# Half of the first layer's cross values computed between the output projection and the expert choice, with the bias table's write and the router's VectorE order moved

## The chip, the cores and the metric

One Trainium2 chip, one of its cores. The metric is the device time of one execution in microseconds (us), the median of several runs. One core has TensorE (PE: matmuls, and PEld: the loads of their stationary operand), VectorE (DVE), ScalarE (ACT), GpSimd (POOL), SyncE (SP, which here only issues transfers) and 16 DMA engines. All tensors are float32.

## The reference, cut to what matters

Two models run one behind the other on a sequence of 256 tokens of width 1024. The first block is a mixer (convolution branch and gated linear attention), then a mixture of 32 experts of width 512, of which the router picks 2 for each token. The second has two layers, each with a feed-forward part, a mixer (RWKV heads and block attention), cross attention to a memory of 256 rows, and a second feed-forward part.

```python
h = x + ga1 * (merged @ w_out)                     # output projection of the first block
t = modulate(rmsnorm(h, g_norm2), sh2, sc2)
lg = t @ w_rg + b_rg                               # router: 4 groups,
le = t @ w_re + b_re                               # 32 experts
...                                                # best group, its two best experts, weights comb
for e in range(N_EXPERTS):
    y = y + comb[:, e:e + 1] * ((silu(t @ w1[e]) * (t @ w3[e])) @ w2[e])
...
# second block, for each of its 2 layers
k, v = split(rms_norm(mem, mem_norm_g[l]) @ w_kv, 2)   # 256 x 1024 each
```

The keys `k` and values `v` of the cross attention depend on `mem` and on weights alone, not on `x`. So they can be made at any time.

## The kernel before, in words

Every engine has a program of its own; they meet at semaphores (`wait_ge`, `then_inc`), and an instruction that waits holds up everything behind it on its engine. The order on each engine is written by hand. There is no scheduler.

**First block.** `tensor1` (PE), `scalar1` (ACT), `vector1` (DVE), `pool1` (POOL) and `sync1` (SP) run the mixer. Its weights come in pieces of 2 MB (`PIECES1`) into a ring of four slots, `ring`; a slot is loaded again once its piece has been read (`read`). At the end stand the output projection (piece `out`, 2 halves of 512 columns, 2 row tiles `t`, 8 matmuls for each: L954), then 16 transposes of the normalised memory (`mem`, L962). DVE adds each result to `x` (L1313, L1315); ACT and POOL make its norm (L234, L248, L250), ACT and DVE scale it into `xs` (L241, L255), PE transposes it (L263), ACT and DVE write `xT` (L279, L287).

**The choice.** `tensor_moe` runs the router (16 matmuls with 36 columns, L1331) and a small matmul for the table of relative position biases (`bydist`, L1338). ACT copies that table (L1069) and POOL writes it to DRAM, once for each of 128 partitions (`bias_dram`, 1.5 MB). DVE turns the router's numbers into the choice (`vector_moe`, L1547 to L1614): some 35 small operations, each waiting for the one before it. Five small matmuls (L1342 to L1346) count the tokens of each expert; DVE tests whether all have at most 64 (`fits`), and all engines branch on it. In the branch that is taken, `tensor_gathered`, DVE makes a one-hot table `hot` (L1659), PE gathers the tokens of two experts with it (`gather`, L1367, 16 matmuls) and zeroes four banks (L1430).

**The experts.** A loop over 16 pairs of experts. For each pair the weights come in 12 pieces of 1 MB (w1, w3, w2 of two experts), 4 into `more` and 8 into the ring. `up` (L1383) reads the first eight, `down` (L1420) the last four. SP may load a piece of the next pair as soon as `up` or `down` has counted it as read (`hid_up`, `hid_down`). The first pair's pieces are loaded ahead, during the mixer's end.

**Second block, mixer of a layer.** `cross_kv(l, g)` makes the cross keys (g = 0 to 3, banks copied to `k_out`) and values (g = 4 to 7, `v_out`, L2179) out of `gm`, the transposed memory with its gain. In `moba_attention` the values fill PE between the eight heads of the block attention: for each head `turned` (L2255, waits for DVE's `probs`), `scores` (L2245), `values` (L2263), then the fill, and for h < 4 `mats` (L2225). ACT's `take_kv` empties the banks; POOL writes keys and values to DRAM (`k_dram`, `v_dram`) and reads them back later.

Of the kernel before, what the change touches and what calls it, by code (L numbers as in the profile page):

```python
# [11 lines left out]
P = 128  # L12
# [16 lines left out]
NH = 8  # L29
# [90 lines left out]
def piece(j, base=(0,) * SLOTS, turn=0):  # L120
# [6 lines left out]
           + [("pw", 0), ("glao", 0), ("glao", 1), ("out", 0), ("out", 1)])  # L127
# [16 lines left out]
def build(nc, a, out):  # L144
    ctx = ExitStack()
    with ctx:
# [223 lines left out]
        bydist = tmp[:, 0, 0:NDIST]  # L370
# [191 lines left out]
        v_dram = nc.dram_tensor("cross_values", (P, NT * D), F32)  # L562
        bias_dram = nc.dram_tensor("bias_by_distance", (NH, P, NDIST), F32)
# [78 lines left out]
        def moe_slot(p):  # L642

            if p < 4:
                return more[:, p, :]
            s = 1 + (p - 4) // 2
            return ring[:, s % SLOTS, (p % 2) * HALF:(p % 2 + 1) * HALF]
# [72 lines left out]
        def pool1(pool):  # L720
# [9 lines left out]
            for t in (QS, KS):  # L730
# [27 lines left out]
            nc.gpsimd.memset(bydist[0:NH, SEQ:NDIST], -BIG).then_inc(bd_ready, 1)  # L758
            pool.dma_start(lc[:, :], a["cols2"][0]).then_inc(lc_loaded, 16)
# [3 lines left out]
            pool.wait_ge(bd_ready, 2)  # L763
            pool.dma_start(bias_dram.ap(), bydist[0:NH, :].unsqueeze(1).to_broadcast([NH, P, NDIST])
                           ).then_inc(bd_stored, 16)
            pool.wait_ge(bd_stored, 16)


        def tensor1(pe):
# [176 lines left out]

            for half in range(2):
                s = wait_piece(pe, J1["out", half])
# [8 lines left out]
            pe.wait_ge(xs_act, N_MEM + 1)  # L957
            pe.wait_ge(xs_dve, N_MEM + 1)
            for b in range(KD // 2):
                for k in (2 * b, 2 * b + 1):  # L960
                    for t in range(NT):
                        last = nc.tensor.transpose(  # L962
                            bank[MEM_BANK[b]][:, (k % 2) * SEQ + t * P:(k % 2) * SEQ + (t + 1) * P],
                            mem[:, t, k * P:(k + 1) * P], eye)
                last.then_inc(tr_full, 1)

# [3 lines left out]
        def scalar1(act):  # L970
# [85 lines left out]
            for t, done in enumerate((xs_act, xs_dve)):  # L1056
                nc.scalar.activation(mem[:, t, :], mem[:, t, :], ACT.Copy, scale=rstd[:, t:t + 1]).then_inc(done, 1)
            act.wait_ge(x_ready, 1)
# [4 lines left out]
            for b, done in enumerate((None, xT_act, None, xT_dve)):  # L1063
                act.wait_ge(tr_full, 8 + b + 1)
                last = nc.scalar.activation(flat(memT[:, 2 * b:2 * b + 2, :]), bank[MEM_BANK[b]][:, :], ACT.Copy)
                if done is not None:
                    last.then_inc(done, 1)
            act.wait_ge(bd_psum, 1)
            nc.scalar.activation(bydist[0:NH, 0:SEQ], bank[6][0:NH, 0:SEQ], ACT.Copy).then_inc(bd_ready, 1)  # L1069
# [254 lines left out]
        def tensor_moe(pe):  # L1324
            norm_transposes(pe, N_ROUTER, 3)

            pe.wait_ge(xT_act, 2)
# [7 lines left out]
            pe.wait_ge(xT_act, 3)  # L1335
            pe.wait_ge(xT_dve, 3)
            pe.wait_ge(mem_loaded, 64)
            nc.tensor.matmul(bank[6][0:NH, 0:NDIST], relT[0:RB, :], onehot[0:RB, :],  # L1338
# [2004 lines left out]
```

## Time and profile before

| | |
|---|---|
| time, median of 3 runs | 2411.93 us (2409.89 to 2412.05) |
| the profiled execution: time | 2405.88 us |
| its span in the profile | 2404.1 us |
| PE busy | 2313.2 us, 96% |
| PEld / DVE / ACT / POOL busy | 65% / 45% / 18% / 2% |
| mean granted TensorE clock | 0.983 |
| HBM read / written | 491.34 MB / 6.82 MB |
| slice 6 of 40 (about 300 to 360 us): PE busy, granted clock | 7 tenths, 7 tenths |
| all later slices: PE busy, granted clock | 8 tenths or more, 9 tenths or more |
| PE idle for expert weights (group L1383, part 5 of the page) | 8.2 us |

PE is busy nearly all the time, so the profile's first part says little. The second part cuts the span into 40 slices of 60 us: there one sees where PE is not busy, where its clock is down, and where the DMA engines run at their top rate of 422 GB/s. The stages are found with the timeline, which lists the instructions of an engine in order of time, with the idle time before each and who ended it.

### The profile page before, as it was taken

What the parts mean: (1) busy time and instruction counts of PE and PEld (TensorE: products, weight loads), DVE (VectorE), ACT (ScalarE), POOL (GpSimd) and SP (SyncE); (2) the same over time, 40 slices, a digit from 0 to 9 for tenths busy, and PEclk for the clock granted to TensorE, in tenths of its full rate; (3) what the DMA queues carried; (4) which work ended last, traced back from release to release, by engine and by line L of the source; (5) the groups of instructions that cost most, each with busy time, mean ns of one, the idle gap of its engine ahead of it and who ended that gap; (6) DMA issues with size and microseconds to landing.
All of it is one profiled execution on the core that took longest, in us unless ns stands there. A gap on an engine that the chain in (4) does not pass through costs nothing. (4 is left out here: it accounts for less than half of the span.)

```text
span 2404.1 us, 28968 instructions
## 1 busy us (share of the span) xinstructions
PE 2313.2 (96%) x12084; PEld 1566.9 (65%) x12084; DVE 1080.3 (45%) x2030; ACT 429.5 (18%) x842; POOL 46.0 (2%) x75
## 2 busy tenths in 40 slices
PE   6999979999999989999999999999999999999998
PEld 4778845444444468758758658847866876776873
DVE  2888321111111176652543346666664255335675
ACT  1122211111111111100322221102100131221110
POOL 1000000000000010000000000000000000000000
PEclk9999979999999999999999999999999999999999
DMA  9566548999999955444330435427444342044541
GB/s 397 235 235 255 233 132 290 422 422 422 422 422 422 407 172 163 175 158 149 119 136 2 172 117 174 161 103 230 160 153 175 123 158 89 32 145 149 175 163 47
DMA packets 175837, 499.74 MB, mean 208 GB/s; under 512 B 6872, under 2 KB 99304, under 8 KB 145776
## 3 DMA queue, kind: packets, MB, share of 16 engines
q1 hardware_dynamic: 171904, 481.23, 53.3%
q0 software_dynamic: 3680, 16.43, 2.3%
q8 instruction: 81, 1.33, 0.2%
q10 hardware_dynamic: 144, 0.52, 0.1%
q14 instruction: 28, 0.23, 0.0%
HBM read 491.34 MB, written 6.82 MB: 207 GB/s over the span
## 5 line engine op out<-in xcount | busy, mean ns | idle before, releaser
L2032 PE MATMUL bank<-Tw,Sx 128*128 128x256 f32 x960 | 213.8, 379 | 0.0
L2032 PEld LDWEIGHTS bank<-Tw,Sx 128*128 128x128 f32 x960 | 179.3, 190 | 22.7
L2120 PE MATMUL bank<-xT,ring 128*128 128x256 f32 x704 | 152.6, 379 | 0.0
L848 PE MATMUL bank<-xT,ring 128*128 128x256 f32 x640 | 143.6, 384 | 2.8 <-ACT xT L279 2.8
L2120 PEld LDWEIGHTS bank<-xT,ring 128*128 128x128 f32 x704 | 133.4, 190 | 18.0
L2032 PE MATMUL bank<-ring,xT 128*128 128x256 f32 x640 | 144.7, 379 | 0.0
L848 PEld LDWEIGHTS bank<-xT,ring 128*128 128x128 f32 x640 | 122.7, 193 | 21.9 <-ACT xT L279 2.9
L2032 PEld LDWEIGHTS bank<-ring,xT 128*128 128x128 f32 x640 | 121.6, 190 | 18.2 <-issue 1.9
L1383 PE MATMUL bank<-ring,xg 128*64 128x512 f32 x512 | 114.6, 594 | 8.2 <-DMA ring<-in_w 8.2
L1420 PE MATMUL bank<-ring,hTg 128*64 128x512 f32 x512 | 113.4, 595 | 0.0
L1383 PE MATMUL bank<-more,xg 128*64 128x512 f32 x512 | 112.6, 592 | 0.0
L2072 PE MATMUL bank<-Tw,Sx 128*128 128x512 f32 x240 | 108.9, 592 | 0.0
L1700 DVE TENSOR_TENSOR sg<-sg,bank 128x512 f32<-128x512 f32 x16 | 11.0, 688 | 215.4 <-PE bank L1383 215.4
L2840 DVE TENSOR_TENSOR whole<-bank,part 128x256 f32<-128x256 f32 (+1 forms) x124 | 53.7, 433 | 100.7 <-PE bank L2032 99.6
L2545 ACT ACTIVATE part<-bank 128x256 f32<-128x256 f32 (+1 forms) x88 | 35.5, 404 | 346.7 <-PE bank L2072 218.4
L1383 PEld LDWEIGHTS bank<-ring,xg 128*64 128x64 f32 x512 | 36.2, 137 | 83.9 <-issue 67.4
L1420 PEld LDWEIGHTS bank<-ring,hTg 128*64 128x64 f32 x512 | 35.3, 137 | 76.1 <-issue 76.1
L1383 PEld LDWEIGHTS bank<-more,xg 128*64 128x64 f32 x512 | 36.7, 137 | 73.3 <-issue 73.3
L2072 PEld LDWEIGHTS bank<-Tw,Sx 128*128 128x128 f32 x240 | 45.6, 190 | 57.4 <-issue 57.4
L2072 PE MATMUL bank<-ring,fh 128*128 128x512 f32 x176 | 82.7, 592 | 0.0
L1705 DVE COPY ye<-bank 128x512 f32<-128x512 f32 x16 | 11.1, 692 | 150.3 <-PE bank L1420 150.3
L2548 ACT ACTIVATE fs<-whole,rstd 128x256 f32<-128x256 f32 x80 | 40.3, 503 | 214.4 <-DVE whole L2840 214.4
(506 smaller groups left out, 3609.6 us busy)
## 6 DMA issues: line engine op xcount, KB each, us to landing
ring<-in_w SPq DMA_DIRECT2D x128, 1024.0 KB, 19.1
ring<-in_ffn_w_in SPq DMA_DIRECT2D x88, 1024.0 KB, 7.7
ring<-in_first_pieces SPq DMA_DIRECT2D x33, 2048.0 KB, 12.0
more<-in_w SPq DMA_DIRECT2D x64, 1024.0 KB, 19.2
ring<-in_ffn_w_out SPq DMA_DIRECT2D x20, 2048.0 KB, 7.9
ring<-in_w_mix_in SPq DMA_DIRECT2D x12, 2048.0 KB, 7.7
ring<-in_xattn_w_kv SPq DMA_DIRECT2D x8, 2048.0 KB, 8.4
ring<-in_w_mix_out SPq DMA_DIRECT2D x4, 2048.0 KB, 10.2
```

The source lines that it names most:

```text
L848: last = nc.tensor.matmul(b[:, c * SEQ:(c + 1) * SEQ], w[:, k, m * P:(m + 1) * P], xT[:, k, :], start=(k == 0), stop=(k == KD - 1))
L1383: last = nc.tensor.matmul(bank[2 + m][e * CAP:(e + 1) * CAP, :], xg[:, 4 * half + k, e * CAP:(e + 1) * CAP], up_rows(4 * m + 2 * half + e) ...
L1420: last = nc.tensor.matmul(bank[half][e * CAP:(e + 1) * CAP, :], hTg[:, c * P + e * CAP:c * P + (e + 1) * CAP], down_rows(8 + 2 * (c // 2) ...
L1700: nc.vector.tensor_tensor(sg[:, 1, :], sg[:, 0, :], bank[3][:, :], ALU.mult).then_inc(h_ready, 1)
L1705: nc.vector.tensor_copy(ye[:, 1, :], bank[1][:, :]).then_inc(ye_dve, 1)
L2032: last = nc.tensor.matmul(bank[BANK_OF[name]][:, 0:SEQ], lhs(k), rhs(k), start=(k == 0), stop=(k == 3))
L2072: return nc.tensor.matmul(bank[BANK_OF[name]][:, :], lhs, rhs, start=(g == 0), stop=(g == FB - 1))
L2120: last = nc.tensor.matmul(b[:, c * SEQ:(c + 1) * SEQ], w[:, k, col:col + P], xT[:, k, :], start=(k == 0), stop=(k == KD - 1))
L2545: nc.scalar.activation(dst, src, ACT.Copy).then_inc(ffn_copied, 1)
L2548: nc.scalar.activation(fs[:, t, :], src, ACT.Silu, scale=rstd[:, t:t + 1]).then_inc(hid_silu, 1)
L2840: return nc.vector.tensor_tensor(dst, a_, b_, ALU.add)
```

## The change

- The weights of values' columns 0 to 511 of layer 0 (2 MB of `xattn_w_kv`) become one more piece of the first block, ("kv", 0), last in `PIECES1`. It sits between the piece of the second `out` half and the experts' first pieces, and moves the ring slot of all later pieces by one. The first pair's pieces 10 and 11 now wait until it has been read.
- The memory's transposes stand between the two halves of the output projection, and the bias table's matmul ahead of the first half. ACT writes the gained memory for these values into free space (`gm_first`: slices of `AT` and `v`) and half of `memT` there.
- PE makes the values of row tile 0 (8 matmuls) ahead of the norm's transposes, 1 matmul of tile 1 between these and the router, the other 7 behind the router. ACT copies both to `v_out`; POOL writes them to DRAM.
- POOL issues the load of `lc` behind the memory's loads, and the bias table's write between the norm of the memory and that of the router's input.
- DVE's three memsets (`y`, `comb`, `place`) stand ahead of its wait for the router. `fits` is computed ahead of `place`, and the first `hot` ahead of the branch. ACT's load of `gf_row` moves behind the exponentials, the values and a wait for the bias table's write (`bd_stored`).
- In layer 0 of the second block only g = 6 and 7 of the values are left to make. They are spread over heads 0 to 6. Layer 1 stays as it was.

```diff
-           + [("pw", 0), ("glao", 0), ("glao", 1), ("out", 0), ("out", 1)])
+           + [("pw", 0), ("glao", 0), ("glao", 1), ("out", 0), ("out", 1), ("kv", 0)])
@@ sync1
+                if PIECES1[j][0] == "kv":
+                    sp.dma_start(slot_w(s, KD, 512), a["xattn_w_kv_2"][0][:, D:D + 512].rearrange(
+                        "(k p) n -> p k n", p=P)).then_inc(w_full[s], 16)
+                    return
...
+                elif kind == "out":
+                    sp.wait_ge(out_psum, 2 * (n + 1))
                 else:
-                    sp.wait_ge(out_psum, 2 * (n + 1))
+                    sp.wait_ge(kv_psum, 2)
@@ pool1
+            pool.dma_start(lc[:, :], a["cols2"][0]).then_inc(lc_loaded, 16)
+            nc.gpsimd.memset(bydist[0:NH, SEQ:NDIST], -BIG).then_inc(bd_ready, 1)
             norm_rstd(pool, N_MEM)
+            pool.wait_ge(bd_ready, 2)
+            pool.dma_start(bias_dram.ap(), bydist[0:NH, :].unsqueeze(1).to_broadcast([NH, P, NDIST])
+                           ).then_inc(bd_stored, 16)
             norm_rstd(pool, N_ROUTER)
...
-            pool.wait_ge(bd_ready, 2)
-            pool.dma_start(bias_dram.ap(), bydist[0:NH, :].unsqueeze(1).to_broadcast([NH, P, NDIST])
-                           ).then_inc(bd_stored, 16)
+            pool.wait_ge(kv_act, 2)
+            pool.dma_start(v_rows[:, :, 0:512], v_out[:, :, 0:512]).then_inc(v_stored, 16)
             pool.wait_ge(bd_stored, 16)
+            pool.wait_ge(v_stored, 16)
@@ tensor1
+            pe.wait_ge(mem_loaded, 64)
+            pe.wait_ge(merged, 1)
+            nc.tensor.matmul(bank[4][0:NH, 0:NDIST], relT[0:RB, :], onehot[0:RB, :],
+                             start=True, stop=True).then_inc(bd_psum, 1)
...
             for half in range(2):
+                if half == 1:
+                    memory()
@@ tensor_moe
+            w = slot_w(wait_piece(pe, J1["kv", 0]), KD, 512)
+            pe.wait_ge(xT_act, 2)
...
+            values(0, range(KD))
             norm_transposes(pe, N_ROUTER, 3)
-            pe.wait_ge(xT_act, 2)
+            values(1, range(1))
+            pe.wait_ge(xT_act, 3)
...
+            values(1, range(1, KD))
...
-            pe.wait_ge(bd_ready, 2)
+            pe.wait_ge(kv_act, 2)
@@ scalar_moe
             act.wait_ge(x_ready, 1)
-            act.dma_start(gf_row[:, :], a["g_final"].partition_broadcast(P)).then_inc(gf_loaded, 16)
+            take_values(0)
...
+            take_values(1)
+            act.wait_ge(bd_stored, 16)
+            act.dma_start(gf_row[:, :], a["g_final"].partition_broadcast(P)).then_inc(gf_loaded, 16)
@@ vector_moe
             dve.wait_ge(x_ready, 1)
+            nc.vector.memset(y[:, :, :], 0.0).then_inc(moe_taken, 1)
+            st(nc.vector.memset(comb[:, :, NE:], 0.0))
+            st(nc.vector.memset(place[:, :, NE:], 0.0))
             dve.wait_ge(router_psum, 1)
...
@@ moba_attention
+                low, high = range(0, 4), range(4, KD)
+                if l == 0:
+                    fill = {0: [(6, low)], 1: [(6, range(4, 6))], 2: [(6, range(6, KD))], 3: [(7, range(0, 2))],
+                            4: [(7, range(2, 4))], 5: [(7, range(4, 6))], 6: [(7, range(6, KD))]}
```

PE, from the output projection to the branch (the same names in both; `bank<-ring,AT` and `bank<-ring,v` of the changed kernel are the new values). Before:

```order
L954 MATMUL bank<-ring,sgT 128x512 x32
L962 MATMUL bank<-K,srT 128x128 x16
L263 MATMUL bank<-K,xs 128x128 x16
L1331 MATMUL bank<-wr,xT 128x36 x16
L1338 MATMUL bank<-v 8x384
L1342 MATMUL bank<-sel,K 128x32
```

Now:

```order
L964 MATMUL bank<-v 8x384
L988 MATMUL bank<-ring,sgT 128x512 x16
L974 MATMUL bank<-K,srT 128x128 x16
L988 MATMUL bank<-ring,sgT 128x512 x16
L1364 MATMUL bank<-ring,AT 128x512 x6
L1364 MATMUL bank<-ring,v 128x512 x2
L263 MATMUL bank<-K,xs 128x128 x16
L1364 MATMUL bank<-ring,AT 128x512
L1377 MATMUL bank<-wr,xT 128x36 x16
L1364 MATMUL bank<-ring,AT 128x512 x5
L1364 MATMUL bank<-ring,v 128x512 x2
L1384 MATMUL bank<-sel,K 128x32
```

The memory's transposes and the bias matmul moved ahead of the last `out` half, and 16 matmuls of 512 columns stand in three places around the norm's transposes and the router.

POOL, from the memory's last load to the second block, in the changed kernel:

```order
L764 DMA K<-in_block_tiles 128x576
L765 DMA lc<-in_cols 128x82
L766 MEMSET v 8x128
L248 TENSOR_SCALAR ms<-ss 128x2 [waits ss_ready]
L250 TENSOR_TENSOR rstd<-ms,neghalf 128x2 [waits ms_ready]
L769 DMA bias_by_distance<-v 1024x1x384 [waits bd_ready]
L248 TENSOR_SCALAR ms<-ss 128x2 [waits ss_ready]
L250 TENSOR_TENSOR rstd<-ms,neghalf 128x2 [waits ms_ready]
L774 DMA lora<-in_rwkv_w_up 64x512 [waits lc_loaded,x_ready]
```

Before, `bias_by_distance` stood five rows later, behind the second norm and the loads of `lc`, `lora` and `gup`.

PE, heads 1 and 2 of the block attention in layer 0 (`K,sm` is `turned`, `km,qm` is `scores`, `pmT,vm` is `values`, `ring,gm` the fill). Before:

```order
L2264 MATMUL bank<-pmT,vm 64x128
L2179 MATMUL bank<-ring,gm 128x512 x4
L2225 MATMUL bank<-kk,aT 128x128 x4
L2255 MATMUL bank<-K,sm 128x128 x3
L2245 MATMUL bank<-km,qm 128x128
```

Now:

```order
L2336 MATMUL bank<-pmT,vm 64x128
L2251 MATMUL bank<-ring,gm 128x512 x2
L2297 MATMUL bank<-kk,aT 128x128 x4
L2327 MATMUL bank<-K,sm 128x128 x3
L2317 MATMUL bank<-km,qm 128x128
```

The fill of a head falls from 4 matmuls to 2 (head 0: from 8 to 4); nothing else of the heads moves.

## Rows read from the trace of the kernel before

**Rows 1.** Timeline of PE, output projection to pair 1: start, duration, instruction, [idle before].

```profile
299.81 27.63 PE L954 MATMUL bank<-ring,sgT 128*128 128x512 f32 x64
327.27 1.91 PE L962 MATMUL bank<-K,srT 128*128 128x128 f32 x16
334.51 3.67 PE L263 MATMUL bank<-K,xs 128*128 128x128 f32 x16 [5.33 <-ACT xs L241]
339.37 7.01 PE L1331 MATMUL bank<-wr,xT 128*128 128x36 f32 x32 [1.18 <-DVE xT L287]
346.31 1.44 PE L1338 MATMUL bank<-v 32*8 32x384 f32 x2
355.44 0.64 PE L1342 MATMUL bank<-sel,K 128*128 128x32 f32 x2 [7.68 <-DVE sel L1614]
...
361.84 6.68 PE L1367 MATMUL bank<-hot,xs 128*128 128x128 f32 x32 [4.06 <-DVE hot L1659]
368.36 3.60 PE L1430 MATMUL bank<-y 128*128 128x512 f32 x8
371.89 7.09 PE L1383 MATMUL bank<-more,xg 128*64 128x512 f32 x32
...
400.60 0.60 PE L1383 MATMUL bank<-more,xg 128*64 128x512 f32 x2
```

**Rows 2.** Windows: busy us of PE, PEld, DVE, ACT, POOL; clock, DMA.

```profile
344.00:346.00 2.00, 2.00 (x12) 2.00 (x11) 0.00 (x0) 0.00 (x0) 0.00 (x0) 0.50 0.00 0
...
366.00:368.00 2.00, 2.00 (x12) 2.00 (x11) 0.00 (x0) 1.98 (x5) 0.00 (x0) 0.54 0.44 46
```

**Rows 3.** Timeline of DVE, router to branch.

```profile
346.49 0.30 DVE L1547 TENSOR_TENSOR lg<-bank,brow 128x36 f32<-128x36 f32 x2 [7.27 <-PE bank L1331]
347.16 1.76 DVE L1549 MEMSET y<- 128x2048 f32 x1 [0.38 <-issue]
...
349.01 0.16 DVE L1557 TENSOR_REDUCE rt<-lg 128x2 f32<-128x8 f32 x1
...
355.19 0.20 DVE L1614 TENSOR_SCALAR sel<-comb 128x64 f32<-128x64 f32 x1
...
358.38 0.15 DVE L1623 TENSOR_SCALAR fits<-most 128x1 int32<-128x1 f32 x1
361.29 0.49 DVE L1659 TENSOR_TENSOR hot<-K,place 128x128 f32<-128x128 f32 x2 [2.76 <-issue]
```

**Rows 4.** Timeline of ACT, first use of the loaded memory.

```profile
292.00 1.06 ACT L1053 ACTIVATE cz<-srT 128x1024 f32<-128x1024 f32 x1 [28.50 <-DMA K<-in_block_tiles]
```

**Rows 5.** Transfers of 346 to 386: size, median us to landing.

```profile
bias_by_distance<-tmp POOLq DMA_DIRECT2D x1, 1536.0 KB, 34.2
```

**Rows 6.** Windows at the start and in the middle of the expert loop.

```profile
375.76:386.00 10.24, 10.24 (x50) 3.41 (x47) 0.11 (x1) 0.60 (x1) 0.00 (x0) 1.00 0.80 195
...
440.00:500.00 60.00, 60.00 (x300) 25.88 (x296) 7.10 (x20) 8.43 (x17) 0.00 (x0) 1.00 1.01 422
```

**Rows 7.** Timeline of PE, the last of nine waits for expert weights.

```profile
822.21 2.37 PE L1383 MATMUL bank<-ring,xg 128*64 128x512 f32 x10 [0.94 <-DMA ring<-in_w]
```

**Rows 8.** Timeline of PE, heads 2, 4 and 5 of layer 0.

```profile
1217.22 0.55 PE L2255 MATMUL bank<-K,sm 128*128 128x128 f32 x3
...
1230.89 0.55 PE L2255 MATMUL bank<-K,sm 128*128 128x128 f32 x3
...
1236.55 0.49 PE L2255 MATMUL bank<-K,sm 128*128 128x128 f32 x3
```

**Rows 9.** Timeline of DVE, probabilities of head 5 of layer 0.

```profile
1235.52 0.35 DVE L3039 TENSOR_SCALAR sm<-sm,small 128x256 f32<-128x256 f32 x1
```

**Rows 10.** Windows of layer 0: light matmuls of the heads, after a wait.

```profile
1296.00:1300.00 4.00, 4.00 (x40) 3.87 (x38) 0.00 (x0) 0.59 (x1) 0.00 (x0) 1.00 0.00 0
1378.00:1379.00 1.00, 1.00 (x5) 0.99 (x6) 0.00 (x0) 0.23 (x3) 0.00 (x0) 0.59 1.08 384
```

**Rows 11.** Timeline of PE, that wait, in the cross attention.

```profile
1377.94 0.93 PE L2462 MATMUL bank<-K,sx 128*128 128x128 f32 x4 [2.63 <-DVE sx L3182]
```

More of the change, by code:

```diff
@@ L956, in tensor1 @@
                     last.then_inc(out_psum, 1)
[L957 to L965, printed above, removed]
         MEM_BANK = (4, 6, 7, 5)
@@ L1057, in scalar1, with memory @@
                 nc.scalar.activation(mem[:, t, :], mem[:, t, :], ACT.Copy, scale=rstd[:, t:t + 1]).then_inc(done, 1)
+            act.wait_ge(bd_psum, 1)
+            nc.scalar.activation(bydist[0:NH, 0:SEQ], bank[4][0:NH, 0:SEQ], ACT.Copy).then_inc(bd_ready, 1)
+            def memory(b):
+                return nc.scalar.activation(flat(memT[:, 2 * b:2 * b + 2, :]), bank[MEM_BANK[b]][:, :], ACT.Copy)
+            act.wait_ge(lc_loaded, 16)
+            for k in range(KD):
+                act.wait_ge(tr_full, 8 + k // 2 + 1)
+                nc.scalar.activation(gm_first[k], bank[MEM_BANK[k // 2]][:, (k % 2) * SEQ:(k % 2 + 1) * SEQ], ACT.Copy,
+                                     scale=column(lc, C2, "mem_g")[:, k:k + 1])
+            memory(0)
+            memory(1).then_inc(xT_act, 1)
             act.wait_ge(x_ready, 1)
@@ L1062, in scalar1 @@
             act.wait_ge(xT_dve, 2)
[L1063 to L1069, printed above, removed]
+            memory(2)
+            memory(3).then_inc(xT_dve, 1)
             return st
@@ L1324, in tensor_moe, with values @@
         def tensor_moe(pe):
+            w = slot_w(wait_piece(pe, J1["kv", 0]), KD, 512)
+            pe.wait_ge(xT_act, 2)
+            def values(t, ks):
+                for k in ks:
+                    last = nc.tensor.matmul(bank[4 + 2 * t][:, :], gm_first[k][:, t * P:(t + 1) * P], w[:, k, :],
+                                            start=(k == 0), stop=(k == KD - 1))
+                if ks[-1] == KD - 1:
+                    last.then_inc(kv_psum, 1)
+            values(0, range(KD))
             norm_transposes(pe, N_ROUTER, 3)
-            pe.wait_ge(xT_act, 2)
+            values(1, range(1))
+            pe.wait_ge(xT_act, 3)
             pe.wait_ge(xT_dve, 2)
@@ L1622, in vector_moe @@
             st(nc.vector.tensor_tensor(place[:, :, 0:NE], place[:, :, 0:NE], sel[:, :, :], ALU.mult))
-            nc.vector.tensor_scalar(fits[:, :], most[:, :], CAP + 0.5, None, ALU.is_lt).then_inc(fits_ready, 1)
+            st.sync()
+            for t in range(NT):
+                last = nc.vector.tensor_tensor(
+                    hot[:, t, :].rearrange("p (e c) -> p e c", e=2),
+                    K[:, DESC, 0:CAP].unsqueeze(1).to_broadcast([P, 2, CAP]),
+                    place[:, t, 0:2].unsqueeze(2).to_broadcast([P, 2, CAP]), ALU.is_equal)
+                if t < NT - 1:
+                    st(last)
+            last.then_inc(hot_ready, 1)
             st.sync()
@@ L1942, in sync2 @@
                 mid += [(a["xattn_w_o_2"], 512 * n, 512) for n in range(2)]
-                js = [j for j in range(J_MIX, J_FFN2) if j not in J_SKIPPED]
-                for j, (w, c, width) in zip(js, mid, strict=True):
+                for j, (w, c, width) in zip(range(J_MIX, J_FFN2), mid, strict=True):
+                    if skipped(l, j):
+                        continue
                     read(l, j - SLOTS)
@@ L2164, in rwkv_operands, with cross_kv @@
                     last.then_inc(lora_psum, 1)
-            def cross_kv(l, g, parts=(0, 1)):
-                if 0 in parts:
+            def cross_kv(l, g, ks=range(KD)):
+                if ks[0] == 0:
                     if g < 2:
@@ L2176, in cross_kv @@
                     t = g % 2
-                    for part in parts:
-                        for k in range(4 * part, 4 * part + 4):
-                            last = nc.tensor.matmul(bank[g % 2][:, :], gm[:, k, t * P:(t + 1) * P], w[:, k, :],
-                                                    start=(k == 0), stop=(k == KD - 1))
+                    for k in ks:
+                        last = nc.tensor.matmul(bank[g % 2][:, :], gm[:, k, t * P:(t + 1) * P], w[:, k, :],
+                                                start=(k == 0), stop=(k == KD - 1))
                 else:
```

91 lines of the change are left out of this document (56 added, 35 removed).

## The prediction

> **What bounds the kernel now.** I began with the page's table: PE is busy for 96% of the span, so time can only come out of the few places where PE waits or runs at the lower of its clock's two levels, or out of stages that something else limits. Slice 6, around 300 to 360 us, is the worst of them: 7 tenths busy at 7 tenths of the clock. The timeline of PE shows what stands there [rows 1]. The output projection ends at 327.4. From there to the first expert matmul at 371.9 PE waits four times: 5.33 us for the norm, 1.18 us, 7.68 us for the choice, 4.06 us for the branch and `hot`. After the first wait the clock is at 0.50, that is 1.2 of 2.4 GHz, and it stays there until about 367.5 [rows 2]. So the norm's 16 transposes take 3.67 us, while the memory's 16 of the same shape took 1.91 us at the full clock, and the gather takes 6.68 us. What sets the end of this stage is a chain, not PE's work: x, norm, transposes, `xT`, router, some 35 small DVE operations, counting, branch, gather.
>
> Next the expert loop. A pair takes 28.7 us on PE (371.89 to 400.60) [rows 1]. Its weights are 12.58 MB, at 422 GB/s [rows 6] 29.8 us. The DMA engines are therefore the slower side, and the loads run behind a lead of one pair. Late in the loop PE waits for weights; the last time is pair 15's second half of w3, at 822.21 [rows 7]. Without any wait that matmul would have stood at 371.9 + 10.4 + 15 x 28.66 = 812.2, so about 10 us are lost to loads. Hence the end of the loop follows the time of the first load of the loop (which starts when `up` of pair 0 has read its first piece, 3.9 us in, at 375.8) and how well the loads run from then on. They run badly at first: 195 GB/s in the first 10.2 us [rows 6]. The bias table's write is in flight then; it is issued behind the bias matmul, which ends at 347.8, and ACT's copy, and lands 34.2 us after its issue [rows 5], so near 383.
>
> In layer 0's block attention PE is busy throughout: 6.84 us for each of the heads 2 and 3 [rows 8].
>
> **The change, step by step, up to the experts.** Times are those of the profiled execution.
>
> Ahead of the projection a matmul of 384 columns is added. It took 1.44 us at the low clock [rows 1]; here 0.7. It needs the memory loads, which landed at 292.0 [rows 4], 8 us before; their queue now has 4 MB less ahead of it. The memory's transposes move in: 1.8. Both were behind the projection, in the shadow of the chain; now they delay it by 2.5. The projection ends at 329.9 and the norm is ready at 334.5 + 2.5 = 337.0.
>
> In that wait lie 8 of the new matmuls: 27.63/32 = 0.86 us each [rows 1], 6.9 in all, so PE is busy until 336.8. ACT's eight gained copies and two copies of `memT` in front of them (10 x about 0.5) lie under the second half, 13.8 us long. Cost nothing; if they were late, PE would wait one for one.
>
> The clock then does not fall before the transposes: 1.9 instead of 3.7. ACT and DVE each make four pieces of `xT` of about 0.5 us, and they end at 340.1; so the router starts at 340.2 (before 339.4). Its 7.01 us at the low clock become about 3.6: it ends at 343.8 instead of 346.4. DVE's memsets (1.76 plus issue, 347.16 to 349.01) no longer stand between router and choice [rows 3]: 1.8 saved. `sel` comes at 355.2 - 2.6 - 1.8 = 350.8 to 351.1. The last 7 new matmuls (6.0) fit from 343.8 to 349.9. Counting takes 1.25 instead of 2.3, `fits` is computed first, so it is ready at 352.8 instead of 358.5. DVE paid 2.76 for its branch ahead of `hot` [rows 3]; now `hot` is made before it, and PE pays only its own branch, 2.8 by the same row. The gather starts at 355.6 instead of 361.8: **6.2 saved**.
>
> Is the gather then faster? PE has done little since 349.9 (ten records of 32 columns) and idles 3.1 us just ahead. A wait of 2.63 us in the cross attention was enough for a fall, to 0.59 in the next microsecond [rows 10, 11]. I take the fall as given and the gather at about 6.6 us. First expert matmul: 365.6, **-6.3**. At the full clock it would be 6.68 x 1.91/3.67 = 3.5, which is 3.1 less: -9.4.
>
> **The loads of the loop.** The bias write is now issued at about 302 and is over near 340, under the projection, where loads have slack of 30 us and more. So the loop's loads begin at full rate. In those 10.2 us only 1.67 MB of weights moved (2.0 less the write's 0.33, that is 7.5 us of its 1.57 MB in 34.2); at 422 GB/s after 1.9 us to start it would be 3.5 MB, 4.4 us more. But then the queue runs dry for about 1.7 us: eight pieces take 8.39/0.422 = 19.9 us, while `down`, the last 7.1 us of the pair before 400.6 and as many matmuls as one `more` half of `up`, releases its first half near 397.4, 21.6 us after the first issue. I take **-2.7**, with bounds 0 and -4.4. The waits for weights, 10 us, are large enough to give it back.
>
> The Trainium skill ("DMA: Bandwidth & Descriptors", Anatomy of one DMA) gives a DMA issued from GpSimd about 2.0 us plus its bytes at 436 GB/s, an estimate of 5.6 us for this table. By that it would have ended long before 375.8, moving it would give nothing, and the sum would be 2.7 less. The trace has 34.2 us, so the row decides.
>
> **Layer 0.** 16 matmuls leave the heads: 16 x 0.86 = 13.8. They are fill; where the heads' own chain is longer, PE now waits. Heads 1 to 3 need 5.1 us of PE each, DVE needs about 5.0 from one `mats` to the next probabilities. For head 5 the DVE chain is visible: `turned` of head 4 starts at 1230.89 and the probabilities of head 5 end at 1235.87 [rows 8, 9], 4.98 later, while PE gets there in 5.66 - 1.72 = 3.94. One wait of 1.0. **-12.7**, bounds -13.8 and -10 (a wait like it at three more heads).
>
> Sum: -6.3 - 2.7 - 12.7 = -21.7. On the profiled 2405.9 (span 2404.1 and 1.8 around it) that is 2384.2; that execution was 6.0 below the median, so 2411.9 - 21.7 = **2390.2**.
>
> **Rivals.**
> A, the clock falls during the router. Its 36 columns for each load of 128 are light work. For: 344 to 346, the same router, fully busy, stayed at 0.50 [rows 2]. Against: in layer 0, 1296 to 1300, matmuls of 64 columns with full weight loads kept 1.00 [rows 10]. Price: router 7.0 again (+3.4), the seven matmuls behind it partly at half speed (+1.7), and PE instead of DVE then decides when counting starts: first expert matmul 2.3 earlier instead of 6.3. Time 2394.2.
> B, the clock holds through to the gather: another 3.1, so 2387.1.
> C, a fill that buys little: the loads keep their slow start for another reason, or the heads of layer 0 are bound by DVE from head to head at 5 us and more. -15, so 2397.
> D, slower: the bias write, now shared with the experts' first pieces, lands late. ACT waits for `bd_stored` ahead of its branch, and `xg`, without which `up` cannot start, is behind that. For: in 375.8 to 386 write and weights did slow each other. Against: alone it took 34.2 us, so from 302 it lands at 336, and ACT needs it only by 355. Beyond that each microsecond delays the experts by one; the 21.7 us are used up at 377, that is 75 us after its issue. At 90 us it would be 15 slower, 2427.
> E, it does nothing: layer 0's heads are bound by DVE alone and the experts' end by loads that start no earlier, because pieces 10 and 11 (issued only when the values are read, at 350) come late for `down`. Against: 34 us lie between 350 and `down`'s first use at 387. 2411.
>
> **How the numbers follow.** Main case 0.52 (its own range 2386 to 2394), A 0.2, B 0.1, C 0.12, D 0.03, E 0.03. The three runs shown lie 2 us apart, and waits such as [rows 11] meet the clock by chance, 1 or 2 us more. 2383 to 2400 leaves out D, E and the outer parts of A, B and C, under 2 in 10. About 0.2% (5 us) is what a measurement of this kernel tells from no change. Faster: 0.94, all of main, A, B, C. Same 0.03, slower 0.03.
>
> **What would show it.** Right: the values' 512-column matmuls between projection and transposes with under 1 us of idle; transposes near 1.9 and router near 3.6 us; `bias_by_distance` issued near 302 and landed before 350; first expert matmul near 365.6 less the profile's own shift; over 400 GB/s in the 10 us behind the first load; waits for weights about 7 us in all; layer 0's eight heads 12 to 13 us shorter, with one wait of 1 us at head 5. Wrong: clock 0.50 in the router, a wait of ACT for `bd_stored`, idle time at more than two heads, or a gap in the loads between `up` and `down` of pair 0 above 3 us.

## The result and the profile after

The changed kernel takes 2385.86 us (median of 4 runs, 2381.41 to 2386.11), the kernel before in the same job 2410.91 (4 runs, 2409.86 to 2412.05). The ratio is 0.9892, with a 95% interval of 0.9875 to 0.9909: 25 us faster, where 21.7 were forecast, and inside the range. The profiled execution took 2381.41 us with a span of 2379.6, against 2404.1.

The timeline of PE over the same stage as [rows 1]:

```profile
299.62 0.81 PE L964 MATMUL bank<-v 32*8 32x384 f32 x2
...
315.94 13.90 PE L988 MATMUL bank<-ring,sgT 128*128 128x512 f32 x32
329.68 5.31 PE L1364 MATMUL bank<-ring,AT 128*128 128x512 f32 x12
334.82 1.88 PE L1364 MATMUL bank<-ring,v 128*128 128x512 f32 x4
336.95 1.97 PE L263 MATMUL bank<-K,xs 128*128 128x128 f32 x16 [0.24 <-ACT xs L241]
...
340.20 3.92 PE L1377 MATMUL bank<-wr,xT 128*128 128x36 f32 x32 [0.42 <-DVE xT L287]
343.92 6.07 PE L1364 MATMUL bank<-ring,AT 128*128 128x512 f32 x10
349.83 1.88 PE L1364 MATMUL bank<-ring,v 128*128 128x512 f32 x4
351.55 0.30 PE L1384 MATMUL bank<-sel,K 128*128 128x32 f32 x2
...
354.33 3.83 PE L1409 MATMUL bank<-hot,xs 128*128 128x128 f32 x32 [1.59 <-DVE hot L1675]
358.00 3.60 PE L1472 MATMUL bank<-y 128*128 128x512 f32 x8
361.53 7.09 PE L1425 MATMUL bank<-more,xg 128*64 128x512 f32 x32
```

The waits of 5.33 and 7.68 us are gone: the values' matmuls (L1364) stand in them. Both transposes and router run at the high clock now. The first expert matmul starts at 361.53, before at 371.89: 10.4 us, where 6.3 were forecast. The row of the gather (L1409) says why it is more: the wait ahead of it is 1.59 instead of 4.06 us, and it takes 3.83 instead of 6.68.

Windows of the same execution (busy us of PE, PEld, DVE, ACT, POOL; granted clock, DMA share, GB/s):

```profile
343.00:348.00 5.00, 5.00 (x15) 2.79 (x15) 3.30 (x21) 0.21 (x1) 0.00 (x0) 0.66 0.25 103
348.00:356.00 8.00, 6.41 (x34) 4.29 (x33) 4.29 (x25) 1.74 (x4) 0.70 (x1) 1.00 0.39 114
365.39:376.00 10.61, 10.61 (x53) 3.75 (x50) 0.47 (x1) 0.60 (x1) 0.00 (x0) 1.00 0.89 356
...
835.00:849.00 14.00, 8.21 (x22) 5.21 (x23) 10.23 (x17) 4.66 (x10) 3.77 (x6) 0.51 0.67 209
1179.00:1184.00 5.00, 4.99 (x26) 4.13 (x27) 4.74 (x12) 0.00 (x0) 0.00 (x0) 0.66 0.00 0
```

The clock did fall, but only as the router ended, at 343.6, and for 3.4 us (0.66 over 343 to 348): rival A in a mild form. It then held at 1.00 to the gather, as rival B has it. The first 10.6 us of the loop's loads ran at 356 GB/s; in [rows 6] all transfers together, the write's among them, ran at 195. The last two rows are falls that cost something later; the one at 1179 is new.

DVE at the branch, to be held against [rows 3]:

```profile
353.00 0.15 DVE L1665 TENSOR_SCALAR fits<-most 128x1 int32<-128x1 f32 x1
...
353.65 0.49 DVE L1675 TENSOR_TENSOR hot<-K,place 128x128 f32<-128x128 f32 x2
355.20 0.48 DVE L1746 MEMSET ye<- 128x512 f32 x1 [1.06 <-issue]
```

The branch cost DVE 1.06 us, no longer 2.76. PE's gather waited for `hot`, which ended at 354.14, so PE's own branch was over by then and did not set the gather's start. The bias table's write, issued at 301.1, as the transfers show it (size, median us to landing; [rows 5] before):

```profile
bias_by_distance<-v POOLq DMA_DIRECT2D x1, 1536.0 KB, 36.1
```

It landed at 337, 7 us before the router's end. Then PE at the end of the experts, and in layer 0's heads:

```profile
808.27 3.65 PE L1425 MATMUL bank<-ring,xg 128*64 128x512 f32 x16 [0.94 <-DMA ring<-in_w]
...
840.11 1.97 PE L302 MATMUL bank<-K,x 128*128 128x128 f32 x8 [8.71 <-DVE x L1698]
...
1188.76 0.49 PE L2327 MATMUL bank<-K,sm 128*128 128x128 f32 x3
...
1206.60 0.55 PE L2327 MATMUL bank<-K,sm 128*128 128x128 f32 x3
...
1211.72 0.55 PE L2327 MATMUL bank<-K,sm 128*128 128x128 f32 x3
...
1216.75 0.55 PE L2327 MATMUL bank<-K,sm 128*128 128x128 f32 x3 [0.93 <-DVE sm L3118]
...
1226.24 1.16 PE L2305 MATMUL bank<-R,aT 64*128 64x128 f32 x16
```

L302, the first work behind the experts, stood at 853.96 before: 13.9 us. Ahead of the first head 10.6 of them are left (before it started at 1199.34), behind the last head there are 23.2 (before 1249.42). So the heads gave 12.6. The end of the span is 24.5 earlier.

### The profile page after: what moved, and what is told of

It reads as the page before. It is cut to its first block and busy times, and to the rows that moved or that the text cites. A ratio compares the mean times of both kernels' runs of the same rounds, so it can differ in the third digit from the quotient of the medians.

```text
span 2379.6 us, 28978 instructions
## 1 busy us (share of the span) xinstructions
PE 2307.9 (97%) x12084; PEld 1560.1 (66%) x12084; DVE 1080.0 (45%) x2030; ACT 432.1 (18%) x850; POOL 47.1 (2%) x76
```

## The experiments

Where executions are compared, times count from S, the start of the bias matmul or of the projection's first matmul, whichever comes first, since executions reach it at different times (299.6 to 305.4). "Branch" is the idle time of DVE at its branch on `fits`.

**e1, the write late again.** Everything else as changed; the table's matmul stands behind the router, the write is issued at 344.7.

```diff
-            pool.wait_ge(bd_ready, 2)              # ahead of norm_rstd(pool, N_ROUTER)
-            pool.dma_start(bias_dram.ap(), ...).then_inc(bd_stored, 16)
...
+            pool.wait_ge(bd_ready, 2)              # behind the LoRA loads
+            pool.dma_start(bias_dram.ap(), ...).then_inc(bd_stored, 16)
             pool.wait_ge(kv_act, 2)
```

> The changed kernel with one part undone: the bias table's matmul, ACT's copy and the write to DRAM stand behind the router again, as before; the load of gf_row is issued by POOL behind that write. The values, VectorE's order and layer 0 are as changed. Theory 1: the write in flight slows both the engines' branch (2.76 us of idle before, 1.06 after) and the first loads of the expert loop (3.5 us). Then the branch is near 2.7 us again, PE's wait at it is long enough for the clock to fall, the gather takes 6.7 instead of 3.8 us, the loads lose 3.5 us: about 8 us slower than the changed kernel, 2394. Theory 2: the branch is short because hot is made ahead of it, and the write costs the loads alone: branch near 1.1 us, gather 3.8 us, 2389 to 2390.

Measured: 2393.61 us (2392.35 to 2395.63, 4 runs), ratio 0.9938 (0.9921 to 0.9954); in this job the kernel before took 2409.67. From DVE, SP and PE of its timeline:

```profile
356.90 0.48 DVE L1744 MEMSET ye<- 128x512 f32 x1 [2.56 <-issue]
```

```profile
368.83 10.33 SPq L707 DMA_DIRECT2D more<-in_w  x4
```

(SP's row in the changed kernel, for comparison: it issues the same first four loads of the loop in 4.26 us.)

```profile
365.39 4.26 SPq L707 DMA_DIRECT2D more<-in_w  x4
```

```profile
356.13 5.46 PE L1409 MATMUL bank<-hot,xs 128*128 128x128 f32 x32 [3.19 <-issue]
...
853.94 1.97 PE L302 MATMUL bank<-K,x 128*128 128x128 f32 x8 [8.63 <-DVE x L1696]
```

T1's mechanism holds: the branch takes 2.56 again, and behind the longer wait the clock falls in the gather. The experts end at 853.94, where they ended before (853.96), though the first expert matmul is 7 us earlier. All of it was lost again to loads. T1's sizes do not hold. Against the changed kernel the experts end 13.6 us later behind S (554.10 against 540.49): 3.2 of them stand ahead of the first load, and 10.4, not 3.5, are lost behind it. The time fits T1's 2394 by luck: the profiled executions are 10.9 us apart, since behind the experts this one met less of the low clock (10.2 us instead of 13.7, and no fall near 1180), and the medians, from two jobs, 7.8.

**e2, the early write alone**, in the kernel before.

```diff
+            pool.wait_ge(bd_ready, 2)              # ahead of norm_rstd(pool, N_ROUTER)
+            pool.dma_start(bias_dram.ap(), ...).then_inc(bd_stored, 16)
...
+            nc.tensor.matmul(bank[4][0:NH, 0:NDIST], relT[0:RB, :], onehot[0:RB, :], ...)  # ahead of "out"
```

> The kernel before with one part of the change alone: the bias table's matmul ahead of the output projection, its write to DRAM issued by POOL ahead of the router's norm, ACT's load of gf_row behind a wait for it. Theory 1 (the write slows branch and loads): branch near 1.1 instead of 2.76 us, first 10 us of the loop's loads above 350 GB/s instead of 195; the end of the experts 5 to 6 us earlier, 2405 to 2406. Theory 2 (it slows the loads alone): branch 2.7 us, 3 to 4 us earlier, 2407 to 2408.

Measured: 2405.17 us (2402.72 to 2407.14, 10 runs), ratio 0.9981 (0.9971 to 0.999). DVE's branch and the first loads:

```profile
364.94 0.49 DVE L1662 TENSOR_TENSOR hot<-K,place 128x128 f32<-128x128 f32 x2 [1.13 <-issue]
```

```profile
378.17 3.73 SPq L697 DMA_DIRECT2D more<-in_w  x3
```

T1 holds: relative to S the experts end 5.6 us earlier than before (548.57 against 554.15), of which 1.6 are the branch and 3.6 the loads. SP issues the four loads in 4.26 us here (7.09 before), and the first 10.2 us of them run at 356 GB/s.

**e3, VectorE's order alone**, in the kernel before: `fits` ahead of `place`, the first `hot` ahead of the branch, the memsets ahead of the router.

```diff
+            nc.vector.tensor_scalar(fits[:, :], most[:, :], CAP + 0.5, None, ALU.is_lt).then_inc(fits_ready, 1)
             for t in range(NT):
                 st(nc.vector.tensor_scalar(place[:, t, 0:NE], ...))
...
-            nc.vector.tensor_scalar(fits[:, :], most[:, :], CAP + 0.5, None, ALU.is_lt).then_inc(fits_ready, 1)
```

> The kernel before with one part of the change alone: VectorE's memsets ahead of its wait for the router, fits ahead of place, the first hot ahead of the branch. Theory 1: memsets give 1.8 us, hot beside the branch 0.5 to 0.7, the branch stays at 2.7 us since the write is in flight: first expert matmul 2.4 us earlier, 2408.5. Theory 2 (the order shortens the branch): 1.7 us more, 2406.8.

Measured: 2409.93 us (2405.56 to 2413.15, 10 runs), ratio 1.0 (0.999 to 1.0009), so neither theory has its time. DVE, SP and PE:

```profile
360.98 0.48 DVE L1698 MEMSET ye<- 128x512 f32 x1 [2.61 <-issue]
```

```profile
373.93 9.39 SPq L697 DMA_DIRECT2D more<-in_w  x3
```

```profile
370.06 5.37 PE L1383 MATMUL bank<-more,xg 128*64 128x512 f32 x24
...
856.21 1.97 PE L302 MATMUL bank<-K,x 128*128 128x128 f32 x8 [8.61 <-DVE x L1650]
```

The branch stays long, 2.61 us, as T1 has it. The first expert matmul is 3.3 us earlier relative to S (68.80 against 72.08), where T1 had 2.4 and T2 4.1; the end of the experts is not earlier (554.95 against 554.15).

**e4, the gap without its fill**: of the 16 matmuls of the values only 2 are made.

```diff
                 for k in ks:
-                    last = nc.tensor.matmul(..., start=(k == 0), stop=(k == KD - 1))
+                    if k == KD - 1:
+                        last = nc.tensor.matmul(..., start=True, stop=True)
```

> The changed kernel with 14 of the 16 new matmuls of the gap left out (so the first 512 columns of layer 0's values are not the reference's); all else as changed. Theory 1: these matmuls are what keeps TensorE's clock up, and they cost nothing. Without them the clock falls in the norm's wait as before: transposes 3.7, router 7.0, gather 6.7 us, first expert matmul 7 to 8 us later than in the changed kernel, 2393 to 2394. Theory 2: the clock is held up by something else, or they cost what they take from PE (0.7 us, by which the values end behind sel): the same time or 0.7 us less, 2385.

Measured: 2387.11 us (2385.13 to 2390.34, 4 runs), ratio 0.9912 (0.9894 to 0.993). PE:

```profile
337.19 3.54 PE L263 MATMUL bank<-K,xs 128*128 128x128 f32 x16 [6.24 <-ACT xs L241]
341.92 5.23 PE L1378 MATMUL bank<-wr,xT 128*128 128x36 f32 x32 [1.18 <-DVE xT L287]
...
354.04 0.61 PE L1385 MATMUL bank<-sel,K 128*128 128x32 f32 x2 [5.03 <-DVE sel L1662]
```

Without the fill the clock falls and PE waits 6.24 and 5.03 us. The first expert matmul is 4.8 us later than in the changed kernel (66.67 against 61.91 behind S) and the experts end 4.7 later. That is T1's mechanism, not its size of 7 to 8 us: router and gather took 5.23 and 5.25 us, not 7.0 and 6.7, since the clock was down for only a part of each. So beside the heads' shorter work, which e4 keeps, the fill is worth the clock that it holds up. The profiled times are 4.0 us apart; the medians, from two jobs, only 1.3, and the intervals of the two ratios overlap. So this reading rests on the traces, not on the times.

**e5, e9, e10: why the write hurts.** e5 issues e1's late write from ScalarE's queue behind its last copy of the values; e9 does so 8 us earlier, so that packets are under way at the branch; e10 is e1 with the table in partitions 64 to 71.

```diff
-            pool.dma_start(bias_dram.ap(), bydist[0:NH, :]...)            # e1
+            act.dma_start(bias_dram.ap(), bydist[0:NH, :]...)             # e5 behind take_values(1), e9 ahead of take_values(0)
...
-        bydist = tmp[:, 0, 0:NDIST]                                       # e1
+        bydist = tmp[64:64 + NH, 0, 0:NDIST]                              # e10
```

> The changed kernel with the bias write late, as in e1, but issued from ScalarE's queue behind its last copy of the values, no longer from GpSimd's. In e1 the branch took 2.56 us (VectorE, before the memset of ye) and the first 10 us of the loop's weights came at 245 GB/s. T1, the write itself (its packets on the DMA engines) slows both: the branch again takes 2.3 to 2.8 us, the first load's 10 us stay under 270 GB/s, the experts end 554 us behind the output projection's start, time 2393 to 2395. T2, the slow branch and the slow loads come of GpSimd's queue (its descriptors are written by software): the branch takes 1.0 to 1.2 us, the loads come at 350 GB/s, the experts end 546 us behind the projection's start, time 2386 to 2388.

> As e5 (bias write late, from ScalarE's queue), but issued some 8 us earlier, right behind ScalarE's copy of the bias table, so that its packets are under way when the engines branch; in e5 they began at 356 us, behind the branch, which took 0.99 us on VectorE. T1, packets of the write in flight slow the branch, whatever queue they come from: it takes 2.3 to 2.8 us, the gather starts some 1.5 us later than in e5 measured from the projection's first matmul (54.8 us there). T2, only GpSimd's software queue slows it: 1.0 to 1.2 us. Both: the first loads are slow again, the experts end 554 to 556 us behind the projection's start.

> As e1 (bias write late, from GpSimd's queue), but the table lies in partitions 64 to 71 of the on-chip memory, no longer in 0 to 7, where the value also lies that every engine reads for the branch. T1, it is the reading of partitions 0 to 7 by the write that slows the reading of that value: the branch takes 1.0 to 1.3 us, the write still about 36 us and the loads stay slow. T2, it doesn't matter where the table lies: the branch takes 2.5 to 2.8 us. T3, the place sets the write's own length too: under 25 us, and faster loads with it.

Measured: e5 2398.39 us (2395.8 to 2401.07, 4 runs), ratio 0.9958 (0.9941 to 0.9974), its interval overlapping e1's, the experts' end 555.13 us behind S; e9 and e10 one execution each, 2394.78 and 2395.05 (the kernel before 2406.5 to 2412.91). e5, queues of 365 to 380 us (packets, MB, share of 16 engines; q10 is ScalarE's queue with the write, q1 the weights):

```profile
q10 hardware_dynamic: 483, 0.74, 43.9%
q1 hardware_dynamic: 220, 1.61, 31.0%
```

and DVE's branch in e5, e9 and e10, in this order:

```profile
355.30 0.48 DVE L1744 MEMSET ye<- 128x512 f32 x1 [0.99 <-DVE hot L1673]
```

```profile
359.63 0.48 DVE L1744 MEMSET ye<- 128x512 f32 x1 [2.55 <-issue]
```

```profile
358.28 0.48 DVE L1745 MEMSET ye<- 128x512 f32 x1 [3.77 <-issue]
```

On the loads e5 decides for T1. From ScalarE's queue too the write is slow: it lands at 394.08, 42.2 us after its issue. All transfers together run at 159 GB/s from 366 to 376; from 365 to 380 the weights have 107 (1.61 MB) and the write 49 (0.74 MB). The write is no faster by itself: 50 GB/s in e9 from 352 to 355, where nothing else is in flight. On the branch its 0.99 looked like T2, but in e5 the write's first packets came after 356, behind the branch. e9, with packets in flight, gives 2.55: the write's packets slow the branch, whatever queue they come from. In the kernel before, theirs were the only packets in flight during DVE's branch (358.4 to 361.3, 49% of the 16 engines' time). That weights in flight do not is seen in e5 itself: from 353 to 355.4 they took 90% of the DMA engines' time. In e9, where the write was further on when the loads began, these were not slow: 362 GB/s in the first 10.2 us, the write's 32 among them. The experts ended 550.15 us behind S, not the 554 to 556 that both theories had. e10 refutes its T1 and T3: 3.77 us, and 40.0 us to landing. The place of the table isn't the cause. Nor is it the fetching of instructions behind the branch, as far as the traces show: no packet of a queue of the kind `instruction` lies in DVE's branch in the kernel before, e1, e3, e9 or e10.

**e7, VectorE's order undone** in the changed kernel, beside **e8, the changed kernel again**.

> The changed kernel with VectorE's order of before (memsets behind the router's bias, fits behind the places, the first one-hot behind the branch). T1, the order is worth its 3.3 us on the path once the bias write is early: first expert matmul 65.2 us behind the projection's bias matmul (61.9 in the changed kernel), experts' end 543.8 behind it, time 2389. T2, the first loads set the end of the experts again, as they did in e3: the experts end at 540.5 as in the changed kernel, time 2386.

> The changed kernel itself, beside the others on the same chip. Both theories: 2381 to 2387; the difference to e6 and e7 is read against this one.

Measured: e7 2388.12 us (2385.99 to 2389.38, 4 runs), ratio 0.9913 (0.9896 to 0.993); e8 2383.73 (2381.09 to 2386.72, 4 runs), ratio 0.9897 (0.9881 to 0.9914). The two intervals overlap, so the traces decide, and for T1: the first expert matmul comes 66.47 us behind S and the experts end 544.85 behind it, 4.4 later than in the changed kernel (540.49; e8 540.29). `sel` comes later, PE waits 1.45 us for it, and the clock falls in the gather (5.55 us), which makes 4.4 out of the order's own 3.3. The same edit was worth nothing in e3.

All these fit one rule. The end of the experts (L302) follows the first load of the loop by a fixed lag, unless the write is still in flight at that load (the column of the write gives its issue):

| kernel | write issued | first load | L302 less first load |
|---|---|---|---|
| before | 348.46 | 375.76 | 478.20 |
| changed | 301.13 | 365.39 | 474.72 |
| changed again (e8) | 304.39 | 368.66 | 474.51 |
| e2 | 305.68 | 378.17 | 474.57 |
| e4 | 301.39 | 370.42 | 474.68 |
| e7 | 302.00 | 370.82 | 474.52 |
| e9 | 347.25 | 372.28 | 480.43 |
| e3 | 349.90 | 373.93 | 482.28 |
| e1 | 344.74 | 368.83 | 485.11 |
| e10 | 344.88 | 370.29 | 486.94 |
| e5 | 351.91 | 365.70 | 489.24 |

With an early write the lag is the same within 0.2 us, wherever the first load stands. With a late one it is 3.5 to 14.5 longer, roughly the more, the sooner the first load comes after the write's issue (27 us in the kernel before, 14 in e5); e1 and e10 lie higher than their 24 and 25 us, and there the values' transfer was slow too (32.9 and 36.6 us to landing, 9.9 in e5), and so was the second of the first pair's last two pieces, which since the change waits for the values and so goes out beside the write (29.0 and 32.2 us, 25.3 in e9, 11.3 in the changed kernel). SP's issuing is slow as well: 9.9 us for the first four loads in e3, 10.3 in e1, 12.4 in e10 and 13.7 in e5, but 4.26 in e9. Which of these delays makes which part of the lag was not separated. PE's waits show how the loss reaches the end: once the lead of the loads is used up, PE waits some 0.94 us in every pair, in the last nine pairs before, the last six in the changed kernel and all fifteen behind the first in e1. So a gain ahead of the loop is lost to the loads.

**e6, the waits that are left, filled**, to see what the later falls of the clock are worth.

```diff
             scatter((PAIRS + 1) % 2, stop=True)
+            for _ in range(8):
+                nc.tensor.matmul(bank[3][:, :], eye, flat(K[:, 0:4, :]), start=True, stop=True)
...
                 mats(l, 0)
+                cross_kv(l, 3, range(6), (0,))
                 mats(l, 2)
-                cross_kv(l, 3)
+                cross_kv(l, 3, range(6, KD), (0,))
+                cross_kv(l, 3, range(KD), (1,))
...
                 queries(3)
+                for _ in range(2):
+                    nc.tensor.matmul(bank[6][:, :], eye, flat(K[:, 0:4, :]), start=True, stop=True)
```

> The changed kernel with TensorE's waits filled: 8 matmuls of 128x512 whose result nobody reads behind the experts' last scatter (a wait of 8.71 us, behind which the clock was low for 13.7 us, 8.0 of them busy), in both layers six of the cross keys' matmuls ahead of the attention's second matrices (waits of 2.45 and 2.44 us on bon), and 2 such matmuls of 128x512 behind the last queries of both cross attentions (waits of 2.63 us, each followed by 3.4 us of low clock). T1, TensorE sets the time at all of them: 4.0 us from the clock behind the experts, 1.7 us from each of the four other spells of low clock (3.4 us at half speed), and 2.4 us from each wait on bon, 15.7 in all: 2370. T2, what TensorE gains ahead of the first head it waits for sm or pmT: 4.0 and twice or four times 1.7, no gain of the waits: 2375 to 2379.

Measured: 2374.21 us (2373.59 to 2375.43, 4 runs), ratio 0.9853 (0.9836 to 0.9869), 9.5 us under e8. PE's timeline:

```profile
847.50 1.10 PE L302 MATMUL bank<-K,x 128*128 128x128 f32 x8 [1.84 <-DVE x L1700]
...
1180.95 2.86 PE L2259 MATMUL bank<-gm,ring 128*128 128x256 f32 x12
1183.73 1.16 PE L2307 MATMUL bank<-aT,kk 64*128 64x128 f32 x16
...
1353.88 0.66 PE L2545 MATMUL bank<-K,sx 128*128 128x128 f32 x4 [0.92 <-DVE sx L3267]
```

Six of the cross keys' matmuls stand where PE waited 2.45 us for `bon`, and none of the falls behind 840 is left before the program's last 6 us, in which PE has no work. From L302 to the end of the span it takes 1526.1 us, e8 1536.1. The time fits neither theory: T1's 15.7 us is more than what came. It was worked out from the changed kernel's first profile; e8's clock was low for only 10.2 us behind the experts (4.9 busy) and didn't fall near 1180, which leaves 12.4. The traces refute T2's mechanism: the first head of layer 0 comes 3.7 us sooner behind L302 than in e8, and 2.3 of them are the wait on `bon`. Behind the experts T1's term was too large: PE gained 1.4 us where half of e8's 4.9 would be 2.4, for the second half of L302 still waits 1.56 us for DVE. This profile also reached S 2.5 us later than e8's, and its clock fell in the gather. In e12, the same kernel, it fell once more behind the experts, from 845 to 853. How much of such chance falls is in each median is open.

**e11, the start filled as well**, beside **e12, e6 again**.

```diff
             ada_columns(0)
+            keep(1)
             ada_partial(2)
             ada_columns(1)
+            keep(1)
             ada_partial(3)
             ada_columns(2)
             ada_columns(3)
+            keep(2)      # matmuls of 128x512 from xs into bank[4], read by nobody
```

> e6 with four more matmuls of 128x512 whose result nobody reads at the start of the program: one ahead of the third and one ahead of the fourth partial sum (waits of 1.99 us on the first pieces), two ahead of the first projection (a wait of 2.83 us on xT). In e6 the clock was low for 13.6 us from 29 to 43 us, 10.8 of them busy. T1, the clock then stays up and the projections start at full speed: 3 to 5 us less than e6 in the same job. T2, the falls at the start come whatever these waits are, or the weights' arrival sets the projections' pace: within 1.5 us of e6.

> e6 once more, beside e11 on the same chip. Both theories: 2372 to 2377; e11 is read against this one.

Measured: e11 2369.29 us (2368.55 to 2370.36, 5 runs), ratio 0.9828 (0.9815 to 0.9842); e12 2371.98 (2371.23 to 2374.79, 5 runs), ratio 0.9841 (0.9828 to 0.9855); the kernel before took 2411.68. The first projections in e11 and then in e12:

```profile
35.65 14.06 PE L869 MATMUL bank<-xT,ring 128*128 128x256 f32 x64 [1.00 <-ACT xT L279]
```

```profile
38.14 16.57 PE L862 MATMUL bank<-xT,ring 128*128 128x256 f32 x64 [2.83 <-ACT xT L279]
```

The same 64 records take 2.5 us less at the kept clock, as T1 has it; the medians differ by 2.7 us, just under its range. The intervals of the two ratios overlap, though not one run of e11 is above the lowest of e12. How much of the 2.7 is the filling's is open: in the profiles e11 reaches S 2.7 us earlier, but its first weights also came 1.4 us earlier (12.37 against 13.75), and its clock fell near 82 and 143, e12's near 251. Both beat the changed kernel, and e11 has the lowest time of all kernels here.

## Why the prediction was right, and where it was off

**The clock up to `sel`: right in its end, by a mixture of cases.** Transposes 1.97 (forecast 1.9), router 3.92 (3.6), `sel` at 350.66 + 0.20 (350.8 to 351.1). The clock fell as the router ended, at 343.6. Rival A priced that at 4 us, since PE and not DVE would then set when counting starts. That much of A came true: counting starts at 351.55, 0.7 behind the end of `sel`. Its price did not, since the low clock lasted 3.4 us and the router itself was done.

**The branch: this step failed.** It was costed at 2.8 us "by the same row", that of [rows 3], as if it were a fixed price. It took 1.06 us on DVE, and PE's gather started 1.2 us behind the end of `fits` (353.15 to 354.33), released by `hot` and not by the branch. The 2.8 us of [rows 3] were the price of a branch beside the late write, which this change removes; the prediction charged the write to the loads alone. e2 shows that moving the write alone does it (1.13), e1 that moving it back undoes it (2.56), e9 that packets of this write in flight are enough (2.55). The gather starts at 354.33, not 355.6: 1.3 us of the gain.

**The gather: this choice failed.** I took the fall as given and 6.6 us; it took 3.83, with 1.59 us of idle time ahead, not 3.1. That is rival B, 2.8 us. It hangs on the branch in part: in e1, with 3.19 us ahead, it took 5.46. But 1.59 isn't safe either; in e6, with the same wait, it took 5.46 too, so that this execution kept the clock was partly luck. 1.3 + 2.8 make up the 4.1 between 6.3 and 10.4.

**The loads: right, a little small.** Forecast -2.7, measured 478.20 - 474.72 = -3.5. 3.78 MB came in the first 10.6 us, 356 GB/s; the working's 3.5 MB in 10.2 us are 343, so its price of the start, 1.9 us, for which it names no row, was about right (3.78 MB at 422 GB/s leave 1.6), while its sign of being right, "over 400 GB/s", contradicts its own working. The waits for weights fell from 8.2 to 5.3 us; I had read 10 for the first. What I didn't see is that this term and the one before it depend on each other: with the write late, the gain ahead of the loop becomes next to nothing by the experts' end (e1: 7 us; e3: 3.3). The sum was near because the change does both at once.

The Trainium skill ("DMA: Bandwidth & Descriptors", Why a DMA increments its semaphore by 16 and not by 1) says that a transfer is split over the largest number of engines, up to 16, that divides the slowest dimension of both patterns; the table's is 8. The traces agree: the write took 47% of the 16 engines' time in the kernel before, from 366.0 to 370.5, and 44% in e5. That weights, split over all 16, then end as late as their packets on the eight crowded ones fits this, but no run here separates it; nor does one say whether the write's own 49 to 50 GB/s come of the number of engines or of reading only eight partitions. The page's price for the whole write, 5.6 us, that the prediction set against the row, does not hold for this transfer: 36.1 and 40.0.

**Layer 0's heads: right.** -12.6 against -12.7, with the one wait of 0.93 us at head 5 that was worked out as 1.0, and heads 1 to 3 at 5.1 us.

**What the sum left out.** -10.4 - 3.5 - 12.6 = -26.5; the span is 24.5 shorter. Behind the heads 1.3 us more were gained, and I did not trace them. Between the experts' end and the first head 3.3 us came back: behind the experts the clock was low for 13.7 us instead of 10.2, and it fell at 1179 behind a wait of 2.45 us, where it held before. These waits are the same in both kernels; which of them meets a fall differs between executions (e8, the same kernel, had no fall at 1180). e6 shows that they can be filled. So the sum came within 2.8 us of the span's 24.5 partly by luck: 4.1 us of gain ahead of the loop were not in it, 0.8 more came from the loads, and the terms that it left out gave 2.0 back.

**The rivals.** C is refuted by e2 (the loads' slow start goes with the write) and by the heads (12.6 us). D: the table's write landed at 337, 14 us before ACT could have waited for it (351.75). E is refuted by the table above: the first load stood 10.4 earlier, and `down` waited for nothing.

## What to carry to other kernels

Before taking work off the chain ahead of a stream of loads, look at what else is on the DMA engines when the stream starts: with the small-row write there, 3.3 and 7 us gained ahead were all lost by the experts' end (e3, e1); with it gone they stayed. Fill a wait of some 2 us or more on PE, with other real work where there is some and with matmuls whose result nobody reads where there is none, since what stands behind it may run at half the clock. And price an edit that moves several things for its interactions: VectorE's order was worth nothing alone (e3) and 4.4 us beside the early write (e7).

## What the runs showed of the hardware

- A write of 1.5 MB in rows of 1.5 KB from 8 partitions took 34 to 40 us from GpSimd's queue and 42 to 43 from ScalarE's (e5, e9), with 41 to 49% of the 16 engines' time, at 49 to 50 GB/s where it was read off (before, e5, e9). In the first 10 us of loads beside it all transfers together moved 156 to 248 GB/s (before, e1, e3, e5, e10), without it 353 to 358; in e9, where most of it was over, 362.
- Loading a value and branching on it took 1.0 to 1.1 us on VectorE, and 2.55 to 3.8 with that write in flight (before, e1, e3, e9, e10). Why is open: neither the queue (e9) nor the table's partitions (e10) is the cause, and weights at 90% of the DMA engines don't do it (e5).
- The clock fell at the end of the router too (343.6), behind 3.9 us of matmuls of 36 columns with 0.42 us of idle time ahead of them.
- With 1.6 to 1.7 us of idle time behind light matmuls the gather ran at either level, 3.83 us in the changed kernel, e8 and e12, 5.46 in e6 and e11.
- While that write was in flight, SP itself took up to 13.7 us to issue four loads (e5) that took it 4.26 in the changed kernel; in e9 it took 4.26 beside the write's last part. Why is open.
